# Two transformer blocks on one core: the norm factors computed on 128x4 instead of 128x512

## The chip, the cores and the metric

The kernel runs on one core of a Trainium2 chip. The metric is the device time of one execution in microseconds (us), the median over several runs; lower is better.

## The reference, cut to what matters

The program is two layers of a first block (retention, state space and forgetting attention side by side), then RWKV, memory attention, a dilated attention and four SwiGLU feed-forward networks, all for one sequence of 512 tokens of 1024 features in f32. What the change touches is the root mean square norm, which comes ahead of nearly every one of these parts:

```python
def _rmsnorm(t, gain=None):
    t32 = t.astype(jnp.float32)
    t32 = t32 * lax.rsqrt(jnp.mean(t32 * t32, axis=-1, keepdims=True) + EPS)
    ...

def swiglu_ffn(x, norm_g, w_in, w_out):
    gate, up = jnp.split(rms_norm(x, norm_g) @ w_in, 2, axis=-1)
    return (jax.nn.silu(gate) * up) @ w_out
```

Each norm needs one number per token, 1/sqrt(mean of squares + EPS): 512 numbers in all. Call it the token's factor.

## The kernel before, in words

Activations lie with the features on the 128 partitions and the tokens along the free dimension: `x` is 128 x 8 x 512. A weight tile is 128 x 1024; it is loaded into a ring of four `raw` buffers, split by ScalarE (ACT) into a rounded high part (`w_hi`, L379) and by VectorE (DVE) into the rest (`w_lo`, L386), two buffers of each, and multiplied by TensorE (PE) in `Linear.pe` (L475): for each of eight k blocks three passes of 512 columns, hi by hi, hi by lo and lo by hi. One such tile takes 24 passes. The parts of a tile are due again as soon as PE has finished the tile two ahead of it: first ACT's `w_hi`, then DVE's `w_lo`, then PE.

All instructions come from stages, each a set of generators that yield a due time. `weave` merges the generators of an engine by due time into one program per engine. So the due times fix the order, and every engine works in that order: an instruction that waits holds back all behind it on its engine.

The factor must stand on all 128 partitions, since DVE multiplies tiles of 128 x 512 by it. It is made in `Rstd` (L663), ten times over the program counting the stage `TwoNorms`:

- the squares of x (or of the mixer's output) are summed over the eight feature blocks by POOL into `square_sums` (L653, L1394), 128 x 512;
- PE multiplies them by a 128 x 128 matrix of ones (L678), which sums over the partitions and writes the sum of each token on every partition, 128 x 512, in a PSUM bank;
- DVE scales and adds EPS (L687), ACT takes the root (L699), DVE the reciprocal (L691), each on 128 x 512. The result is `rstd`.

At the start of the program the sums are taken otherwise (`Startup.pe`, L927): the eight blocks of squares are multiplied by the ones one after the other, accumulated in the bank. There, DVE also works through the eight loads of the modulation weights `ada` (`Modulation`, L1036 and L1039), PE sums these over the partitions (L1071), and then the first norm is applied (`NormIn`, L1098 and L1106) and the first weight tile can start.

`TwoNorms` (L706) makes the factor of the last norm of the first block and of the norm behind it in one go: two products by the ones (L721), then on DVE and ACT a chain of nine instructions on 128 x 512, with two roots (L764, L767) and two reciprocals (L734, L744). It runs beside four short weight tiles of the memory's keys and values (256 columns to a pass instead of 512).

In each layer of the first block `Layer` puts an `Rstd` between the state space part and the attention `Fox`; the first transposes of the attention's values (`Turns`, L1649, copied out by DVE at L1678) wait for DVE's L687 of it. At the head of layer 1 (`rstd1`) nothing else is left to do while the factor is made. The other five stand at the head of the RWKV projection, of two feed-forward networks, of the keys and of the queries; there PE goes on with the product, since the factor is applied to its result, and the first result is taken late (`NORM_LATE`).

A second group of norms, in `Ret`, works another way: L1958 multiplies the squares as the stationary operand by one column of ones, which gives 128 x 4 (a token to a partition), L1994 and L2047 take root and reciprocal on 128 x 4, and L1967 multiplies a column of this, repeated 128 times as the stationary operand, by the identity, which spreads the factors over the partitions again.

Of the kernel before, what the change touches and what calls it, by code (L numbers as in the profile page):

```python
# [147 lines left out]
N_ROUNDED = CONST["ident"][0]  # L148

# [513 lines left out]
class Rstd(Stage):  # L663

    def __init__(self, core, at, summed, dst, n=T, src=None, bank=None, in_bank=False):
        self.core, self.start, self.summed, self.dst, self.n = core, at, summed, dst, n
        self.bank = bank or core.aux[0]
        self.src = src if src is not None else core.ss[0]
        self.in_bank = in_bank  # L670
        self.total = core.share("rstd_total", 0 if in_bank else 1)
        self.meaned, self.rooted, self.made = (core.share("rstd_" + s, 1) for s in ("mean", "root", "made"))

    def pe(self, pe):
        def sums():
# [4 lines left out]
        return () if self.in_bank else (sums(),)  # L680

    def dve(self, dve):
        def factors():
            r = self.dst[:, 0:self.n]
            yield self.start + 1.0
            dve.wait_ge(*(self.summed if self.in_bank else self.total.ge(1)))
# [7 lines left out]
    def act(self, act):  # L694
        def roots():
            r = self.dst[:, 0:self.n]
            yield self.start + 1.8
            act.wait_ge(*self.meaned.ge(1))
            act.activation(r, r, ACT.Sqrt).then_inc(*self.rooted.inc())  # L699
        return (roots(),)  # L700
# [5 lines left out]
class TwoNorms(Stage):  # L706

    def __init__(self, core, at, summed, apply_at):
        self.core, self.start, self.summed, self.apply_at = core, at, summed, apply_at  # L710
        self.total, self.meaned, self.rooted, self.made, self.applied = (
            core.share("rstd_" + s, n) for s, n in (("total", 2), ("mean", 2), ("root", 2), ("made", 5),
                                                    ("applied", KD)))

    def pe(self, pe):
        def sums():
            core = self.core
# [3356 lines left out]
```

## Time and profile before

| | us |
|---|---|
| median of 3 runs | 3478.35 |
| lowest and highest of them | 3477.93, 3479.72 |
| span of the profiled execution, first to last instruction | 3482.5 |
| PE busy in it | 3349.0 |
| DVE busy in it | 1780.3 |
| ACT busy in it | 1196.0 |
| mean granted clock of PE | 0.978 of full |

The profiled execution is one of its own; of its time the span alone is known, and that is 4.15 us above the median. Times in the rows are us from the start of that span, durations of one instruction in ns where a row says min/median/max. A f32 product is recorded as two passes, so that eight products of one column stand as x16. A clock of 1.00 is 2.4 GHz, one of 0.50 is 1.2 GHz.

### The profile page before, as it was taken

Reading aid. Unit: us, or ns where it says so; the run is one execution under the profiler, and the core shown is the slowest. Engines: PE = TensorE matmul, PEld = TensorE weight load, DVE = VectorE, ACT = ScalarE, POOL = GpSimd, SP = SyncE. Lnnn points to the kernel's source line nnn. Section 1 sums busy time; section 2 is a strip of 40 time slices with the busy share of each in tenths; the row PEclk is TensorE's granted clock in tenths of the full one; section 3 lists DMA queues with packets and bytes.
Section 4 is the critical chain, followed back from the end, with each engine's and each line's share of the span. In section 5 each row is a group of like instructions: output and inputs, shape, how many; then the busy total and the mean of one; then the engine's idle time right before and its main releaser. Section 6 shows DMA issues by size and latency. Waiting matters only on the chain.

```text
span 3482.5 us, 44013 instructions
## 1 busy us (share of the span) xinstructions
PE 3349.0 (96%) x18330; PEld 2599.3 (75%) x18330; DVE 1780.3 (51%) x2532; ACT 1196.0 (34%) x1884; POOL 409.8 (12%) x318
## 2 busy tenths in 40 slices
PE   5999999899999899999999999999999999999999
PEld 4766678576677788887777777888777887678887
DVE  6854454744436743336767554434454335463433
ACT  3344432433443422224333242222353224342221
POOL 0000011000000311002322111100101011011110
PEclk8999999999999999999999999999999999899999
DMA  5631123221222333333200014332322332013332
GB/s 208 212 110 62 51 97 96 67 85 55 61 80 81 101 92 96 93 97 109 68 14 2 26 51 123 92 97 85 102 80 86 96 89 90 10 61 97 91 97 85
DMA packets 83909, 295.44 MB, mean 85 GB/s; under 512 B 9472, under 2 KB 12800, under 8 KB 81664
## 3 DMA queue, kind: packets, MB, share of 16 engines
q1 hardware_dynamic: 78384, 270.61, 25.3%
q10 hardware_dynamic: 5328, 22.02, 1.9%
q8 instruction: 146, 2.39, 0.3%
q14 instruction: 51, 0.42, 0.0%
HBM read 283.94 MB, written 8.65 MB: 84 GB/s over the span
## 4 chain that ended last, share of the span: by engine, by line
PE 83%; DVE 8%; ACT 2%; issue 1%; POOL 1%; DMA 1%; DVEq 0%; POOLq 0%; ACTq 0%
PE acc L475 66%; PE acc L1464 1%; DVE w_lo L386 1%; PE acc L3217 1%; PE acc L2443 1%; DVE square_sums L2902 1%; PE aux L3181 1%; PE aux L1745 1%; PE aux L3186 1%; PE acc L1776 1%; DMA late_ada<-in_ada 1%; ACT w_hi L379 1%; DVE ssd_ex L1366 1%; PE acc L2447 1%; PE acc L2433 1%
## 5 line engine op out<-in xcount | busy, mean ns | idle before, releaser
L475 PE MATMUL acc<-op_hi,w_hi 128*128 128x512 f32 x2624 | 1100.4, 419 | 37.1 <-DVE w_lo L386 16.6
L475 PE MATMUL acc<-op_lo,w_hi 128*128 128x512 f32 x2624 | 1041.7, 397 | 0.0
L475 PE MATMUL acc<-op_hi,w_lo 128*128 128x512 f32 x2624 | 1040.9, 397 | 0.0
L379 ACT ACTIVATE w_hi<-raw 128x1024 fp32r<-128x1024 f32 (+2 forms) x476 | 494.7, 1039 | 1581.6 <-PE acc L475 1549.6
L386 DVE TENSOR_TENSOR w_lo<-raw,w_hi 128x1024 fp32r<-128x1024 f32 (+2 forms) x476 | 576.6, 1212 | 288.5 <-ACT w_hi L379 288.1
L475 PEld LDWEIGHTS acc<-op_hi,w_hi 128*128 128x128 f32 x2624 | 495.9, 189 | 219.2 <-issue 82.4
L475 PEld LDWEIGHTS acc<-op_hi,w_lo 128*128 128x128 f32 x2624 | 496.0, 189 | 120.3
L475 PEld LDWEIGHTS acc<-op_lo,w_hi 128*128 128x128 f32 x2624 | 496.8, 189 | 115.5 <-issue 11.5
L475 PE MATMUL acc<-ffn_hi,w_hi 128*128 128x512 f32 x800 | 316.5, 396 | 0.0
L475 PE MATMUL acc<-ffn_lo,w_hi 128*128 128x512 f32 x800 | 316.1, 395 | 0.0
L475 PE MATMUL acc<-ffn_hi,w_lo 128*128 128x512 f32 x800 | 316.1, 395 | 0.0
L594 DVE SCALAR_TENSOR_TENSOR x<-acc,x 128x512 f32<-128x512 f32 x112 | 77.4, 691 | 286.8 <-PE acc L475 286.7
L815 POOL TENSOR_TENSOR ffn_gate<-ffn_gate,rstd 128x512 f32<-128x512 f32 x66 | 114.8, 1740 | 836.5 <-ACT ffn_gate L806 836.5
L795 DVE TENSOR_TENSOR ffn_product<-ffn_gate,acc 128x512 f32<-128x512 f32 x88 | 60.4, 686 | 260.3 <-PE acc L475 256.1
L475 PEld LDWEIGHTS acc<-ffn_lo,w_hi 128*128 128x128 f32 x800 | 150.2, 188 | 36.8 <-issue 0.2
L475 PEld LDWEIGHTS acc<-ffn_hi,w_hi 128*128 128x128 f32 x800 | 150.2, 188 | 36.6 <-issue 0.2
L475 PEld LDWEIGHTS acc<-ffn_hi,w_lo 128*128 128x128 f32 x800 | 150.2, 188 | 36.4
L790 DVE TENSOR_TENSOR ffn_gate<-acc,rstd 128x512 f32<-128x512 f32 x66 | 45.6, 691 | 183.9 <-PE acc L475 183.8
L1264 ACT ACTIVATE ssd_ex<-aux,ssd_ncum 128x512 f32<-128x512 f32 (+3 forms) x128 | 62.4, 522 | 85.9 <-PE aux L1450 85.9
L1366 DVE TENSOR_TENSOR ssd_ex<-ssd_ex,ssd_cb 128x1024 f32<-128x1024 f32 (+1 forms) x64 | 60.2, 949 | 47.2 <-ACT ssd_ex L1264 47.1
L815 POOL TENSOR_TENSOR ffn_gate<-ffn_gate,square_sums 128x512 f32<-128x512 f32 x22 | 40.0, 1816 | 275.4 <-ACT ffn_gate L806 275.4
L653 POOL TENSOR_TENSOR square_sums<-square_sums,squares 128x512 f32<-128x512 f32 x35 | 56.2, 1604 | 95.9 <-ACT squares L632 95.9
(578 smaller groups left out, 3901.6 us busy)
## 6 DMA issues: line engine op xcount, KB each, us to landing
raw<-in_w SPq DMA_DIRECT2D x436, 512.0 KB, 3.6
late_ada<-in_ada ACTq DMA_DIRECT2D x32, 512.0 KB, 4.4
raw<-in_w SPq DMA_DIRECT2D x32, 384.0 KB, 3.0
ada<-in_ada ACTq DMA_DIRECT2D x4, 1024.0 KB, 15.0
ada<-in_ada SPq DMA_DIRECT2D x4, 1024.0 KB, 21.9
x_mid<-x SPq DMA_DIRECT2D x16, 256.0 KB, 3.4
x<-x_mid SPq DMA_DIRECT2D x2, 2048.0 KB, 9.1
skew<-rel_rows SPq DMA_DIRECT2D x12, 192.0 KB, 3.0
```

The source lines that it names most:

```text
L379: act.activation(self.w_hi[g % 2][:, 0:k, :], self.raw[s][:, 0:k, :], ACT.Copy).then_inc(self.split_hi.handle, 1)
L386: dve.tensor_tensor(self.w_lo[g % 2][:, 0:k, :], self.raw[g % RING][:, 0:k, :], self.w_hi[g % 2][:, 0:k, :].bitcast(F32), ALU.subtract).th ...
L475: mm = pe.matmul(self.bank(s, g), w[:, k, :], a[:, k, 0:s.n], start=(k == 0 and q == 0), stop=(k == k_tiles - 1 and q == 2))
L594: dve.scalar_tensor_tensor(out=x[:, u, :], in0=bank, scalar=self.scale(u), in1=x[:, u, :], op0=ALU.mult, op1=ALU.add).then_inc(core.freed[ ...
L653: pool.tensor_tensor(core.ss[i][:, :], core.ss[i][:, :], src, ALU.add).then_inc(*self.summed.inc())
L790: dve.tensor_tensor(f.gate[:, slot, :], bank, f.rstd, ALU.mult).then_inc(freed, 1)
L795: dve.tensor_tensor(f.product[:, slot, :], f.gate[:, slot, :], bank, ALU.mult).then_inc(freed, 1)
L815: pool.tensor_tensor(f.gate[:, q % 2, :], f.gate[:, q % 2, :], f.rstd, ALU.mult).then_inc(*f.gated.inc())
L1264: act.activation(self.ex[u % self.EX][:, e, 0:n], core.aux[2 * (u % 2) + e][:, 0:n], ACT.Exp, bias=self.ncum[:, b, 2 * pair + e:2 * pair + ...
L1366: dve.tensor_tensor(ex, ex, tiled(cb[pair // 4][:, at[b]:at[b] + n], 2), ALU.mult).then_inc(*self.weighted.inc())
L1464: mm = pe.matmul(core.acc[2 + pair % 2][e * HD:(e + 1) * HD, b * P:T], self.xdt[:, b, h * SSD_DIM:(h + 1) * SSD_DIM], self.ex[u % self.EX] ...
L1745: pe.matmul(core.aux[e][:, 0:n], self.q[half[e], j, t * P:n], self.k[half[e], j, 0:n], start=True, stop=False, skip_group_check=True)
```

## The change

All ten factors are made on 128 x 4. PE multiplies the squares as the stationary operand by one column of ones, four times for the four blocks of 128 tokens; ACT takes the root with scale 1/D and EPS as its bias; DVE takes the reciprocal; PE multiplies a repeated column by the identity, four times, into the same bank; DVE copies the bank to `rstd`, 128 x 512. DVE's L687 is gone. At the start of the program the 32 one-column products accumulate in four columns. `TwoNorms` does its whole chain on 128 x 4 and spreads and copies two results. The identity is loaded in the early transfer with the ones. In the layers the attention's score stage, no longer its transposes, waits, and for the finished factor.

```diff
 class Rstd(Stage):
     def pe(self, pe):
         def sums():
             yield self.start
             pe.wait_ge(*self.summed)
-            pe.matmul(self.bank[:, 0:self.n], self.core.c("ones"), self.src[:, 0:self.n], start=True,
-                      stop=True).then_inc(*self.total.inc())
+            for t in range(NT):
+                mm = pe.matmul(bank[:, t:t + 1], self.src[:, t * P:(t + 1) * P], core.c("ones")[:, 0:1], start=True,
+                               stop=True)
+            mm.then_inc(*self.total.inc())
+        def spreads():
+            yield self.start + 2.6
+            pe.wait_ge(*self.inverted.ge(1))
+            for t in range(NT):
+                mm = pe.matmul(bank[:, t * P:(t + 1) * P], column(core.norm_small[:, t:t + 1]), core.c("ident"),
+                               start=True, stop=True)
+            mm.then_inc(*self.spread.inc())
     def act(self, act):
+            yield self.start + 1.0
+            act.wait_ge(*(self.summed if self.in_bank else self.total.ge(1)))
+            act.activation(core.norm_small[:, 0:NT], self.bank[:, 0:NT], ACT.Sqrt, scale=1.0 / D,
+                           bias=core.norm_eps[:, 0:1]).then_inc(*self.rooted.inc())
     def dve(self, dve):
-            yield self.start + 1.0
-            dve.tensor_scalar(r, self.bank[:, 0:self.n], 1.0 / D, EPS, ALU.mult, ALU.add
-                              ).then_inc(*self.meaned.inc())
+            yield self.start + 2.0
+            dve.wait_ge(*self.rooted.ge(1))
+            dve.reciprocal(core.norm_small[:, 0:NT], core.norm_small[:, 0:NT]).then_inc(*self.inverted.inc())
             yield self.start + 4.0
-            dve.wait_ge(*self.rooted.ge(1))
-            dve.reciprocal(r, r).then_inc(*self.made.inc())
+            dve.wait_ge(*self.spread.ge(1))
+            dve.tensor_copy(self.dst, self.bank[:, :]).then_inc(*self.made.inc())
...
 class TwoNorms(Stage):
+        def spreads():
+            yield self.start + 6.0
+            pe.wait_ge(*self.step.ge(5))
...
 class Startup(Stage):
-            at, n = CONST["ones"]
+            at, n = CONST["ident"][0], EARLY
             sp.dma_start(core.const[:, at:at + n], core.dram["const"][:, at:at + n]).then_inc(*self.ones.inc(16))
...
-                mm = pe.matmul(self.core.aux[0][:, :], self.core.c("ones"), self.core.squares[:, j, :],
-                               start=(j == 0), stop=(j == KD - 1))
+                for t in range(NT):
+                    mm = pe.matmul(self.core.aux[0][:, t:t + 1], self.core.squares[:, j, t * P:(t + 1) * P],
+                                   self.core.c("ones")[:, 0:1], start=(j == 0 and t == 0),
+                                   stop=(j == KD - 1 and t == NT - 1), skip_group_check=True)
...
-        fox.turn_v.ready.append(self.rstd.meaned.ge(1))
+        fox.heads.ready.append(self.rstd.ready())
...
-    rstd0 = Rstd(core, 2.9, startup.summed.ge(1), core.rstd, in_bank=True)
+    rstd0 = Rstd(core, 4.1, startup.summed.ge(1), core.rstd[:, :], in_bank=True)
```

Three places show how the order moves. First DVE at the start of the program, before (`ada_69` to `ada_73` are the first five loads of modulation weights):

```order
L1036 TENSOR_SCALAR ada_sum_77<-ada_69,cond 128x1024
L1039 SCALAR_TENSOR_TENSOR ada_sum_77<-ada_69,cond,ada_sum_77 128x1024
L1039 SCALAR_TENSOR_TENSOR ada_sum_77<-ada_70,cond,ada_sum_77 128x1024 x2
L687 TENSOR_SCALAR rstd<-aux 128x512
L1039 SCALAR_TENSOR_TENSOR ada_sum_77<-ada_71,cond,ada_sum_77 128x1024 x2
L691 RECIPROCAL rstd<-rstd 128x512
L1039 SCALAR_TENSOR_TENSOR ada_sum_77<-ada_72,cond,ada_sum_77 128x1024 x2
L1036 TENSOR_SCALAR ada_sum_78<-ada_73,cond 128x1024
```

and now:

```order
L1077 SCALAR_TENSOR_TENSOR ada_sum_77<-ada_70,cond,ada_sum_77 128x1024 x2
L1077 SCALAR_TENSOR_TENSOR ada_sum_77<-ada_71,cond,ada_sum_77 128x1024 x2
L712 RECIPROCAL norm_small<-norm_small 128x4
L1077 SCALAR_TENSOR_TENSOR ada_sum_77<-ada_72,cond,ada_sum_77 128x1024 x2
L715 COPY rstd<-aux 128x512
L1074 TENSOR_SCALAR ada_sum_78<-ada_73,cond 128x1024
```

The small reciprocal stands where the large one stood, ahead of the work on `ada_72`; the copy stands behind that work. Then DVE in `TwoNorms`, before:

```order
L731 TENSOR_SCALAR rstd<-aux 128x512
L565 TENSOR_TENSOR mem_v_141<-acc,mem_part_149 128x256
L386 TENSOR_TENSOR w_lo<-raw,w_hi 128x1024
L734 RECIPROCAL rstd<-rstd 128x512
L736 TENSOR_TENSOR square_sums<-rstd 128x512
L738 SCALAR_TENSOR_TENSOR square_sums<-aux,square_sums 128x512
L741 TENSOR_SCALAR square_sums<-square_sums 128x512
L565 TENSOR_TENSOR mem_v_141<-acc,mem_part_149 128x256
L386 TENSOR_TENSOR w_lo<-raw,w_hi 128x1024
L565 TENSOR_TENSOR mem_k_140<-acc,mem_part_149 128x256
L744 RECIPROCAL square_sums<-square_sums 128x512
L746 TENSOR_TENSOR square_sums<-rstd,square_sums 128x512
```

and now:

```order
L566 TENSOR_TENSOR mem_v_141<-acc,mem_part_149 128x256
L387 TENSOR_TENSOR w_lo<-raw,w_hi 128x1024
L769 RECIPROCAL norm_small<-norm_small 128x4
L771 TENSOR_TENSOR norm_small<-norm_small 128x4
L566 TENSOR_TENSOR mem_v_141<-acc,mem_part_149 128x256
L387 TENSOR_TENSOR w_lo<-raw,w_hi 128x1024
L775 COPY rstd<-aux 128x512
L566 TENSOR_TENSOR mem_k_140<-acc,mem_part_149 128x256
L775 COPY square_sums<-aux 128x512
L387 TENSOR_TENSOR w_lo<-raw,w_hi 128x1024
```

Between two splits `w_lo` there now stand small instructions and at most two copies. Last PE at the norm inside layer 0, before and now:

```order
L678 MATMUL aux<-square_sums,const 128x512
L475 MATMUL acc<-op_hi,w_hi 128x512
L475 MATMUL acc<-op_lo,w_hi 128x512
L475 MATMUL acc<-op_hi,w_lo 128x512
L1649 MATMUL aux<-const,fox_v 128x128 x4
L475 MATMUL acc<-op_hi,w_hi 128x512
```

```order
L683 MATMUL aux<-const,square_sums 128x1 x4
L476 MATMUL acc<-op_hi,w_hi 128x512
L476 MATMUL acc<-op_lo,w_hi 128x512
L476 MATMUL acc<-op_hi,w_lo 128x512
L1687 MATMUL aux<-const,fox_v 128x128 x4
L476 MATMUL acc<-op_hi,w_hi 128x512
L476 MATMUL acc<-op_lo,w_hi 128x512
L476 MATMUL acc<-op_hi,w_lo 128x512
L691 MATMUL aux<-const,norm_small 128x128 x4
L476 MATMUL acc<-op_hi,w_hi 128x512
```

The spreads stand behind six more weight passes and four transposes; at the five later heads nine weight passes lie between sums and spreads, in `TwoNorms` 51, at the head of layer 1 none. On ACT the root stands directly behind the squares, ahead of the next `w_hi`, at every head; in `TwoNorms` one `w_hi` stands between the two roots.

## Rows read from the trace of the kernel before

**Rows 1.** The page: busy time by engine, and the chain by engine.

```profile
PE 3349.0 (96%) x18330; PEld 2599.3 (75%) x18330; DVE 1780.3 (51%) x2532; ACT 1196.0 (34%) x1884; POOL 409.8 (12%) x318
PE 83%; DVE 8%; ACT 2%; issue 1%; POOL 1%; DMA 1%; DVEq 0%; POOLq 0%; ACTq 0%
```

**Rows 2.** By tile, `rstd`: ns min/median/max, first and last start, form.

```profile
L687 DVE TENSOR_SCALAR rstd<-aux x9: 683/691/692, 22.9 to 3114.4; 128x512 f32<-128x512 f32 x9
L699 ACT ACTIVATE rstd<-rstd x9: 617/631/633, 23.6 to 3117.5; 128x512 f32<-128x512 f32 x9
L691 DVE RECIPROCAL rstd<-rstd x9: 3343/3346/3353, 26.0 to 3118.1; 128x512 f32<-128x512 f32 x9
```

**Rows 3.** By tile, `roots`: the norms of `Ret` on 128x4.

```profile
L1994 ACT ACTIVATE roots<-sums x8: 205/206/208, 526.4 to 1114.1; 128x4 f32<-128x4 f32 x8
L2047 DVE RECIPROCAL sums<-roots x8: 166/168/170, 528.5 to 1114.6; 128x4 f32<-128x4 f32 x8
```

**Rows 4.** Chain of waits, 484 to 532 us: start, us, what.

```profile
487.83 0.86 PE aux L1926 x2
...
525.40 0.79 PE aux L1958 x8
...
530.97 0.89 PE aux L1967 x8
```

**Rows 5.** Timeline of DVE at the start: start, us, instruction, idle before.

```profile
20.41 2.60 DVE L1039 SCALAR_TENSOR_TENSOR ada_sum<-ada,cond,ada_sum 128x1024 f32<-128x1024 f32 x2 [7.02 <-DMA ada<-in_ada]
...
29.31 2.51 DVE L1039 SCALAR_TENSOR_TENSOR ada_sum<-ada,cond,ada_sum 128x1024 f32<-128x1024 f32 x2
31.73 0.74 DVE L1036 TENSOR_SCALAR ada_sum<-ada,cond 128x1024 f32<-128x1024 f32 x1
```

**Rows 6.** Timeline of PE at the start.

```profile
13.20 8.88 PE L927 MATMUL aux<-squares,const 128*128 128x512 f32 x16 [13.20 <-ACT squares L904]
...
44.06 3.57 PE L1071 MATMUL acc<-const,ada_sum 128*128 128x1 f32 x16 [8.55 <-DVE ada_sum L1039]
```

**Rows 7.** Windows: busy PE, PEld, DVE, ACT, POOL, then PEclk, DMA share, GB/s.

```profile
44.00:47.70 3.70, 3.57 (x16) 3.49 (x16) 2.30 (x4) 0.00 (x0) 0.00 (x0) 0.50 0.40 116
47.70:54.30 6.60, 4.66 (x11) 3.18 (x12) 6.44 (x11) 5.34 (x8) 0.00 (x0) 0.50 0.28 94
```

**Rows 8.** Chain of waits at the head of layer 1, 604 to 630 us.

```profile
614.17 2.09 PE aux L678 x2
...
617.67 3.37 DVE rstd L691
...
621.06 0.76 DVE squares L1098
```

**Rows 9.** Chain of waits in `TwoNorms`, 1185 to 1215 us.

```profile
1194.38 3.27 DVE rstd L734
...
1201.35 3.27 DVE square_sums L744
```

**Rows 10.** Timeline of PE in `TwoNorms`.

```profile
1201.08 0.49 PE L475 MATMUL acc<-mem_hi,w_hi 128*128 128x256 f32 x1 [3.61 <-DVE w_lo L386]
...
1206.53 0.39 PE L475 MATMUL acc<-mem_hi,w_hi 128*128 128x256 f32 x1 [0.84 <-DVE w_lo L386]
```

**Rows 11.** Timeline of ACT in `TwoNorms`.

```profile
1192.06 1.06 ACT L379 ACTIVATE w_hi<-raw 128x1024 fp32r<-128x1024 f32 x1 [1.03 <-PE acc L475]
```

**Rows 12.** Timelines in layer 0: PE's first transpose, DVE's first copy of one.

```profile
348.83 0.63 PE L1649 MATMUL aux<-const,fox_v 128*128 128x128 f32 x4 [0.19 <-DVE rstd L687]
...
349.57 0.69 DVE L1678 COPY fox_vtok<-aux 128x512 f32<-128x512 f32 x1 [0.88 <-PE aux L1649]
```

**Rows 13.** Windows at the head of a feed-forward network, columns as above.

```profile
2083.00:2098.00 15.00, 15.00 (x65) 11.70 (x64) 9.43 (x11) 6.53 (x8) 1.31 (x2) 1.00 0.27 81
```

**Rows 14.** Timelines at the queries (PE) and at the RWKV projection (POOL).

```profile
2926.73 0.47 PE L475 MATMUL acc<-op_hi,w_hi 128*128 128x512 f32 x1 [1.13 <-DVE b_q L565]
...
1596.96 2.66 POOL L2798 MEMSET x<- 128x3072 f32 x1 [10.75 <-DMA x_mid<-x]
```

More of the change, by code:

```diff
@@ L710, in __init__ @@
         self.core, self.start, self.summed, self.apply_at = core, at, summed, apply_at
[L711 to L712 removed]
+        self.total, self.rooted, self.step, self.spread, self.made, self.applied = (
+            core.share("rstd_" + s, n) for s, n in (("total", 1), ("root", 2), ("step", 5), ("spread", 2), ("made", 2),
                                                     ("applied", KD)))
     def pe(self, pe):
+        core = self.core
         def sums():
[L717 removed]
             yield self.start
@@ L725, in dve @@
+        return sums(), spreads()
     def dve(self, dve):
+        core = self.core
+        small = core.norm_small
+        first, second, both = small[:, 0:NT], small[:, NT:2 * NT], small[:, 2 * NT:3 * NT]
         def factors():
-            core = self.core
-            first, second, both = core.rstd[:, :], core.ss[0][:, :], core.ss[1][:, :]
-            yield self.start + 1.0
-            dve.wait_ge(*self.total.ge(2))
-            dve.tensor_scalar(first, core.aux[0][:, :], 1.0 / D, EPS, ALU.mult, ALU.add).then_inc(*self.meaned.inc())
@@ L740, in factors @@
-            dve.wait_ge(*self.made.ge(3))
-            dve.tensor_scalar(second, second, EPS, None, ALU.add).then_inc(*self.meaned.inc())
-            yield self.start + 9.0
-            dve.wait_ge(*self.rooted.ge(2))
-            dve.reciprocal(second, second).then_inc(*self.made.inc())
-            dve.wait_ge(*self.made.ge(4))
-            dve.tensor_tensor(both, first, second, ALU.mult).then_inc(*self.made.inc())
+            yield self.start + 2.0
+            dve.wait_ge(*self.rooted.ge(1))
@@ new lines, in factors @@
+            dve.reciprocal(first, first).then_inc(*self.step.inc())
+            dve.wait_ge(*self.step.ge(1))
+            dve.tensor_tensor(second, first, first, ALU.mult).then_inc(*self.step.inc())
+            dve.wait_ge(*self.step.ge(2))
+            dve.tensor_tensor(second, second, core.aux[0][:, NT:2 * NT], ALU.mult).then_inc(*self.step.inc())
+            yield self.start + 4.0
+            dve.wait_ge(*self.rooted.ge(2))
+            dve.reciprocal(second, second).then_inc(*self.step.inc())
@@ L748, in final_norm @@
+            dve.wait_ge(*self.step.ge(4))
+            dve.tensor_tensor(both, first, second, ALU.mult).then_inc(*self.step.inc())
+            for i, dst in enumerate((core.rstd[:, :], core.ss[1][:, :])):
+                yield self.start + 8.0 + i
+                dve.wait_ge(*self.spread.ge(i + 1))
+                dve.tensor_copy(dst, core.aux[i][:, :]).then_inc(*self.made.inc())
         def final_norm():
-            core = self.core
             for j in range(KD):
```

81 lines of the change are left out of this document (44 added, 37 removed).

## The prediction

> **What bounds the kernel now.** I began with the page's busy times: PE is busy 96% of the span, DVE 51%, ACT 34%, and the chain that ended last runs 83% over PE and 8% over DVE [rows 1]. So DVE time saved is worth nothing on average, and PE time added costs its full length wherever PE has no gap. The answer hangs on which of the ten norms sits where PE waits. For that I took the durations of the old instructions by tile [rows 2], the same forms on 128x4 from the retention norms, which already work the new way [rows 3, 4], and then each of the ten places by timeline or chain. They fall into four kinds:
>
> - the start, where DVE works from 20.41 us on without a gap [rows 5] and PE waits for it;
> - the head of layer 1, where every step of the norm is on the chain [rows 8];
> - the two norms beside the memory's keys, where DVE's two reciprocals hold back a `w_lo` each and PE idles 3.61 and 0.84 us for these [rows 10];
> - the others, where PE multiplies on. A window at the head of a feed-forward network shows PE busy 15.00 of 15.00 us [rows 13].
>
> **Prices.** Removed from DVE per norm: 0.69 (scale and EPS) and 3.35 (reciprocal); ACT's root of 0.63 becomes 0.21; the small reciprocal costs 0.17 [rows 2, 3]. A copy of 128x512 out of PSUM costs 0.69 [rows 12]. DVE saves 4.04 - 0.17 - 0.69 = 3.18 us per norm. PE at full clock: one f32 product of 512 columns is 0.86 (I take a product of the same form, L1926), four of one column 0.79, four spreads 0.89 [rows 4]. PE pays 0.79 + 0.89 - 0.86 = 0.82 us more per norm. Both new forms are rows of this kernel, so these prices are safe to some 0.1 us each.
>
> **The start.** The sums were 16 passes and took 8.88 us from 13.20 [rows 6], over at 22.1, ahead of DVE's need. They become 64 one-column passes. Which clock do they get? After 13.20 the old passes of 512 columns ran, and the granted clock was full for a while. But one-column passes have their own row: from 44.06 they fill 3.57 us without a gap, at a granted clock of 0.50 (1.2 GHz), and the clock stays at 0.50 through the next window, up to 54.3 [rows 6, 7]. So I take it that they don't raise it: 16 passes are 3.57, four such groups 14.3, and 13.9 when the three inner tails overlap. The early transfer grows by 64 KB and pushes x by about 0.15 (64 KB at the 420 GB/s that the trace shows there). Sums end at 13.35 + 13.9 = 27.25. Root and reciprocal follow with three hops of 0.03: 27.7. DVE has finished `ada_71` at about 25.6 and waits 1.8 us there, behind which all its modulation work is queued; then `ada_72` 2.51, then the copy 0.69, whose spreads (1.8 us at half clock) are hidden behind `ada_72`. The next piece starts at 30.9 instead of 31.73 [rows 5]: **-0.9 us**. If the clock rose, DVE would keep 3.18 less 0.15: that is the lower bound -3.0. The upper bound is +0.5, if a pass costs 0.235.
>
> [...]
>
> **The head of layer 1.** All of this is at half clock: L678 took 2.09 for what is 0.86 at full clock [rows 4, 8]. From 614.17: eight passes are half of 3.57, 1.8; root 0.21, reciprocal 0.17 and hops, to 616.45; spreads twice 0.89, 1.8, to 618.3; copy 0.69, to 619.1. Before, the first tile of `squares` began at 621.06: **-1.9 us**. A clock that comes back earlier could add up to -0.8, which I leave to the range.
>
> **The two norms.** The second `w_lo` there had its `w_hi` ready at about 1195.9 and ran behind the 3.27 us of the first reciprocal and three more full-width steps [rows 9]; PE stood 3.61 us, lost its clock over it, ran the next short tile with starts 0.21 apart where 0.114 is the pace before, and stood again 0.84 us for the `w_lo` behind the second reciprocal [rows 10]. With the change the second `w_lo` ends at about 1197.1. PE pays 16 one-column passes instead of 1.72 us (even) and 16 spread passes of 1.78. Two weight tiles at 2.74 each and the spreads between start the next tile at 1199.1, not 1201.08; that tile takes 2.74 at full clock, so the tile behind it starts at 1201.9 instead of 1206.53 [rows 10]. Its own `w_lo` is done at 1201.7: PE's `w_hi` at 1199.3 plus 1.06, plus 1.22, which leaves 0.2 us. **-4.6 us**. Bounds: -2.0 if only the first gap is paid back and a later split is late, -4.9 with nothing late at all. The spreads must find their columns ready: the second root waits behind the `w_hi` of 1192.06 to 1193.12 [rows 11], the last step is done at 1194.8, and the spreads come up on PE, 51 passes after the sums, at 1195.4. There is 0.6 us to spare.
>
> **Both layers' inner norm.** PE pays 0.82 and gets back the 0.19 for which its first transpose waited for DVE's scaling [rows 12]. The reciprocal does hold DVE's split, but PE had no gap over 0.1 us from it. **+0.6 twice, +1.3**. Bounds 0 and +1.7.
>
> **The heads with PE dense.** A feed-forward network twice and the keys: +0.82 three times [rows 13], **+2.5**. DVE's 3.18 less is worth nothing there, being hidden under PE, whose tiles take 5.6 us each. Bounds +1.8 and +3.
>
> **The queries and the RWKV projection.** At the queries PE stood 1.13 us because the first result could be read only behind the reciprocal [rows 14]. That wait goes, PE's 0.82 comes in its place: **-0.3**. At the RWKV projection PE waits for DVE, and DVE for POOL, whose clearing of x waits until 1596.96 for the store of x [rows 14]; that store is issued behind a weight load that needs a `w_lo` which the norm never delayed. So the date stays and hides PE's 0.82: **0**.
>
> **The sum.** -0.9 - 1.9 - 4.6 + 1.3 + 2.5 - 0.3 = **-3.9 us**. The profiled execution has a span of 3482.5, so 3478.6 by this working; the median of the runs lies 4.15 below that span, and I take the difference over to it: 3478.35 - 3.9 = **3474.4 us**. About 0.2% (7.0 us) is what a measurement of this kernel can tell from no change; the forecast lies inside that.
>
> **The rivals.**
>
> *The one-column sums do get the full clock at the start.* For it: the clock was full from 16.8 to 27 in the old run, and 64 passes last much longer than the 16 of 44.06. Against: that row [rows 6, 7]. The start gives -3.0 in place of -0.9: 3472.3.
>
> *More comes back than I count.* In the layers the chain ran over the reciprocal, the split and the copies behind it, and I call that free; and the head of layer 1 may regain its clock sooner. -0.6 per layer and -0.8, with the full start on top half of the time: 3478.35 - 7 = 3471.3.
>
> *Another split is late in the two norms.* DVE still works in order there: a copy of `rstd` stands behind a tile result that PE delivers only at 1199.3, and the next `w_lo` behind that. With 0.2 us to spare, a hop or two more and a PE that stands again give -2.0 instead of -4.6: 3477.0.
>
> *PE waits for the small reciprocal.* This ends slower. The spreads stand in PE's own order, with the weight passes queued behind them. Between sums and spreads are nine passes, 2.1 us, against 0.5 for root and reciprocal. It decides when the reciprocal comes over 2.1 us late: if ACT's root is behind a table load of 1.28 and a `w_hi` of 1.06, or DVE behind a `w_lo` of 1.22, it is 0.5 + 2.34 - 2.1 = 0.75 us per head, and 1.5 with both. At seven heads 0.75 is +5.2: 3479.6, slower than before, and with both 3484.8. Against: the order shows the root ahead of the next `w_hi` at every head, and the small reciprocal ahead of the `w_lo`.
>
> **How the numbers follow.** Forecast 0.58; full clock at the start 0.13; more comes back 0.10; a late split 0.12; PE waits 0.07. The range 3470 to 3480 holds all but the far ends of the second and the last rival. Faster by over 0.2% needs -7.0: most of the case of more, a part of the full clock, little of the forecast's own spread: 0.18. Slower by over 0.2% needs both delays of the last rival: 0.03. Within: 0.79.
>
> **What would show each step.** At the start, DVE idle some 1.8 us before a reciprocal of 0.17 at 27.5, and PE's 64 passes 0.21 us apart; starts 0.11 apart would mean the first rival. At the head of layer 1, 5.0 us from the sums' start to the first `squares`, not 6.9. In the two norms, no PE gap over 1 us behind a `w_lo` and no drop of the clock there. At the dense heads, PE still without a gap, later by 0.8. Wrong would be: a PE gap before any spread, or a `w_lo` waiting behind a copy.

## The result, and the profile after

| | before | after |
|---|---|---|
| median us (number of runs) | 3479.03 (4) | 3420.85 (4) |
| lowest, highest | 3477.93, 3481.28 | 3415.27, 3432.71 |
| ratio to before, 95% interval | | 0.9841, 0.9822 to 0.9860 |
| profiled execution: own time, span | span 3482.5 | 3432.71, 3430.7 |
| mean granted clock of it | 0.978 | 0.980 |

The change saves 58 us. The forecast was 4. Nothing of that size can lie in ten norms that cost a few us each, so the first question was where in the program the time goes. The page, to be read against [rows 1]:

```profile
PE 3310.2 (96%) x18526; PEld 2629.9 (77%) x18526; DVE 1745.3 (51%) x2533; ACT 1193.3 (35%) x1884; POOL 411.6 (12%) x318
PE 84%; DVE 8%; ACT 2%; issue 2%; POOL 1%; DMA 0%; DVEq 0%; POOLq 0%; ACTq 0%
```

PE is 39 us less busy, though it has 196 more instructions. PE's groups by line show where. Before:

```profile
L475 PE MATMUL acc<-op_hi,w_hi 128*128 128x512 f32 x2624 | 1100.4, 419 | 37.1 <-DVE w_lo L386 16.6 <-DVE op_lo L1106 11.0 <-ACT ssd_soft L1235 3.8
L475 PE MATMUL acc<-op_lo,w_hi 128*128 128x512 f32 x2624 | 1041.7, 397 | 0.0
L475 PE MATMUL acc<-ffn_hi,w_hi 128*128 128x512 f32 x800 | 316.5, 396 | 0.0
```

and after:

```profile
L476 PE MATMUL acc<-op_hi,w_hi 128*128 128x512 f32 x2624 | 1088.8, 415 | 32.7 <-DVE w_lo L387 18.3 <-DVE op_lo L1144 7.0 <-ACT ssd_soft L1273 3.8
L476 PE MATMUL acc<-op_lo,w_hi 128*128 128x512 f32 x2624 | 1029.9, 392 | 0.0
L476 PE MATMUL acc<-ffn_hi,w_hi 128*128 128x512 f32 x800 | 311.4, 389 | 0.0
```

The same passes, the same counts, and each is 4 to 7 ns shorter, also the 800 on `ffn_hi`, nearly half of which lie over 100 us away from any norm. Durations overlap here, so the pace is better read as passes in a stretch. The windows from 2150 to 2400 us, weight passes alone (columns: PE busy, PEld busy, PEclk, DMA share, GB/s), before:

```profile
2150.00:2400.00 250.00, 249.81 (x1071) 200.90 (x1070) 1.00 0.32 95
```

and after:

```profile
2150.00:2400.00 250.00, 250.00 (x1105) 207.01 (x1104) 1.00 0.30 94
```

```text
span 3430.7 us, 44407 instructions
## 1 busy us (share of the span) xinstructions
PE 3310.2 (96%) x18526; PEld 2629.9 (77%) x18526; DVE 1745.3 (51%) x2533; ACT 1193.3 (35%) x1884; POOL 411.6 (12%) x318
## 4 chain that ended last, share of the span: by engine, by line
PE 84%; DVE 8%; ACT 2%; issue 2%; POOL 1%; DMA 0%; DVEq 0%; POOLq 0%; ACTq 0%
PE acc L476 66%; PE acc L1502 1%; DVE w_lo L387 1%; PE acc L3255 1%; PE acc L2481 1%; PE aux L3219 1%; DVE square_sums L2940 1%; PE aux L1783 1%; PE aux L3224 1%; PE acc L1814 1%; ACT w_hi L380 1%; DVE ssd_ex L1404 1%; PE acc L2485 1%; PE acc L2471 1%; PE aux L1801 1%
## 5 line engine op out<-in xcount | busy, mean ns | idle before, releaser
L476 PE MATMUL acc<-op_hi,w_hi 128*128 128x512 f32 x2624 | 1088.8, 415 | 32.7 <-DVE w_lo L387 18.3
L476 PE MATMUL acc<-op_hi,w_lo 128*128 128x512 f32 x2624 | 1030.5, 393 | 0.0
L476 PE MATMUL acc<-op_lo,w_hi 128*128 128x512 f32 x2624 | 1029.9, 392 | 0.0
```

Source lines behind the costliest of these rows:

```text
L476: mm = pe.matmul(self.bank(s, g), w[:, k, :], a[:, k, 0:s.n], start=(k == 0 and q == 0), stop=(k == k_tiles - 1 and q == 2))
```

## The experiments

Runs of the kernel before stood beside each set on the same chip; their medians were 3472 to 3473 us there. Where a window is shown, it is that of 2150 to 2400 us again, weight passes alone.

### One cause at a time: the address without the change, the change without the address

The kernel before, with 64 bytes of padding (e1):

```diff
         core.rstd = core.sb("rstd", [P, T])
+        core.sb("pad", [P, 16])
```

> The kernel before with 64 unused bytes on each partition behind rstd, so that square_sums and every tile behind it lie 64 bytes higher, as in the change; no instruction differs. In the trace of before, a weight pass of 512 columns starts 233.3 ns after the last, in the trace of the change mostly 226.7 ns. Theory A (the addresses do it: the operands of the passes start at a multiple of 128 bytes now, at an odd multiple of 64 before): pace 226.7 ns, and about the time of the change plus the 3.9 us that I had worked out for the norms, 3415 to 3437 us. Theory B (the new instructions set another rhythm on TensorE, the addresses do nothing): 3479 us, pace 233.3 ns.

Measured: 3423.73 us (3414.28 to 3432.09, 4 runs), ratio 0.9851 [0.982, 0.9881], mean pace 227.58 ns.

```profile
2150.00:2400.00 250.00, 250.00 (x1105) 207.01 (x1104) 1.00 0.31 94
```

An allocation that nobody reads or writes gives the gain, with not one new instruction. The changed kernel with its two small tiles in free columns of `roots`, so that all placed tiles lie as before (e2):

```diff
-        core.norm_small, core.norm_eps = core.sb("norm_small", [P, 3 * NT]), core.sb("norm_eps", [P, 1])
+        core.norm_small, core.norm_eps = core.roots[:, 16:16 + 3 * NT], core.roots[:, 16 + 3 * NT:17 + 3 * NT]
```

> The change with its 52 bytes of small tiles put into unused columns of the tile roots, so that all other tiles keep the addresses of before; the same instructions in the same order. Theory A: the passes go back to 233.3 ns, and what is left is the norm change alone, which I forecast at 3474.4 us (3470 to 3480). Theory B: 3415 to 3433 us as the change, pace 226.7 ns.

Measured: 3477.15 us (3469.32 to 3482.54, 10 runs), ratio 1.0004 [0.9991, 1.0017], pace 233.29 ns.

```profile
2150.00:2400.00 250.00, 250.00 (x1073) 201.40 (x1073) 1.00 0.29 93
```

All ten new norms are in it and nothing is gained. Theory A holds, B falls.

### How far: 128 bytes

The changed kernel with 64 bytes more (e3), and the kernel before with 128 (e4):

```diff
+        core.sb("pad", [P, 16])   # changed kernel
+        core.sb("pad", [P, 32])   # kernel before
```

> The change with 64 more unused bytes, so that the operands of the passes start at an odd multiple of 64 bytes again, but 128 bytes above their place in before. Theory A in its form 'multiple of 128 bytes': 233.3 ns and some 3475 us, as with the small tiles in roots. Theory A in another form (some one address, or the place of the small tiles, was bad in before): 226.7 ns and 3415 to 3433 us. Theory B: 3415 to 3433 us.

> The kernel before with 128 unused bytes, operands at an odd multiple of 64 bytes as in before, 128 bytes higher. A control. Theory A, multiple of 128 bytes: 3479 us, 233.3 ns. Theory A in another form: may be 3420 to 3437 us. Theory B: 3479 us.

Measured: 3433.19 us (3428.56 to 3442.72, 4 runs), ratio 0.9882 [0.9856, 0.9908], and 3437.33 us (3433.63 to 3440.59, 4 runs), ratio 0.9891 [0.9864, 0.9917]; paces 229.34 and 229.25 ns. I had thought of a plain rule, that tiles want to begin at a multiple of 128 bytes or must not; it falls, since +128 is quick too, but less than +64.

### Period, and whose address

The operands 256 bytes later; the weights 64 later with the operands fixed; both 64 later; the upper half of the map (with `ffn_hi`, `ffn_lo`) alone 64 later:

```diff
+        core.sb("pad", [P, 64])               # e5, behind rstd

         self.piece = 0
+        self.sb("pad", [P, 16])               # e6 and e7, ahead of raw
         self.raw = [self.sb(f"raw{s}", [P, KC, P]) for s in range(RING)]
...
+        core.cond = core.roots[:, 48:48 + KD] # e6: makes room, so that the operands stay
+        core.att_small = core.roots[:, 32:44]
+        core.sb("pad2", [P, 8])

-        return self.nc.alloc_sbuf_tensor_at(name, shape, dtype, offset=self.at + int(kb * 1024))
+        return self.nc.alloc_sbuf_tensor_at(name, shape, dtype, offset=self.at + int(kb * 1024) + (64 if kb >= 0 else 0))   # e8
```

> The kernel before with 256 bytes of padding per partition, so that every placed tile and with it the operands of the weight passes lie 256 bytes later. So far: +0 gives 233.3 ns from start to start of a pass, +64 gives 227.6, +128 gives 229.3. If the pattern repeats every 256 bytes or less, this is the kernel before again: 233.3 ns, 3473 to 3479 us. If it does not (a period of 512 or more, or only the old place is slow), passes are quicker: 227 to 231 ns and 3415 to 3455 us.

> The kernel before with raw, w_hi, w_lo and the constants 64 bytes later and the operands (op_hi, op_lo, ffn_hi, ffn_lo) and square_sums at their old addresses. Theory 1, the operand's own address sets the pace: 233.3 ns per pass, 3473 to 3479 us, no change. Theory 2, the distance between operand and weight tile sets it (two reads that meet): the distance is 64 bytes off as in the padded kernel, with the other sign, so 227 to 230 ns and 3415 to 3440 us.

> The kernel before with everything in SBUF from the raw weight tiles on 64 bytes later, so that weights and operands keep their distance. Theory 1, the operand's own address: as the kernel with 64 bytes of padding ahead of the operands alone, 227.6 ns and 3415 to 3435 us. Theory 2, the distance: as before, 233.3 ns and 3473 to 3479 us.

> The kernel before with only the upper part of the placed tiles 64 bytes later: ffn_hi, ffn_lo and all that shares their room move, x, squares, op_hi and op_lo stay. If each tile's own address sets the pace of its passes: passes on ffn_hi and ffn_lo at 226.7 ns, those on op_hi and op_lo at 233.3; of some 10,280 passes 2,400 read the ffn tiles, so 2,400 x 6.6 ns = 16 us less, about 3457 to 3463 us. If what else runs beside the passes (writes of x, sums of squares, DVE and ACT in their tiles) sets it, the paces of both kinds move together: all at 233 or all at 227 to 230.

Measured: e5 3469.55 us, ratio 0.9991 [0.9976, 1.0006], 233.29 ns; e6 3470.11, 0.9994 [0.998, 1.0009], 232.64 ns; e7 3475.4, 1.0011 [0.9997, 1.0024], 233.28 ns; e8 3460.65, 0.9965 [0.9952, 0.9979], 231.62 ns in the mean.

- e5: 256 bytes later is as if nothing were moved. The pattern repeats at 256 bytes or a divisor of it, and the divisors 128 and 64 are excluded by the runs above.
- e7: the operands are 64 bytes later as in the quick kernel, but the weights moved with them, and nothing is gained. So it isn't the operand's own address.
- e6: the distance changed the other way and gave nothing, which misses what theory 2 expected there, but is no contradiction once a distance has its own pace each.
- e8: passes on `ffn_hi` and `ffn_lo` at 226.8 and 226.7 ns, on `op_hi` and `op_lo` at 233.3 and 233.2, in one kernel. 2,397 x 6.6 ns is 16 us; measured 11.4 against before's 3472.09. What moves is a property of the pair of tiles that a pass reads.

In e8's window the two kinds are mixed; 1079 lies between, as most tiles there read `op`:

```profile
2150.00:2400.00 250.00, 250.00 (x1079) 202.56 (x1080) 1.00 0.31 96
```

### The distance, tested where it must be quick

Call distance the start of `op_hi` less that of `w_hi`, modulo 256. It is 192 before, 0 in the changed kernel. The kernel that decides (e9) has the operands where they were, modulo 256, and the distance 0 by the weights alone:

```diff
+        self.sb("pad", [P, 48])               # ahead of raw: weights +192
...
+        core.sb("pad2", [P, 16])              # behind rstd: operands +256 in all
```

> The kernel before with raw, w_hi, w_lo and constants 192 bytes later and the placed tiles 256 bytes later. Moving the operands by 256 alone changed nothing (233.3 ns, 3469.6 us); moving the weights by 64 with the operands fixed, or both by 64, changed nothing or little (232.6 and 233.3). Distance theory: what counts is the distance from weight tile to operand modulo 256 bytes; it is 192 in the kernel before, 0 with the operands alone 64 later (226.7 to 227.6 ns), 64 with them 128 later (229.3), 128 in the kernel with the weights alone moved. Here it is 0 again, with the operands at their old place modulo 256: 227 to 228 ns and 3415 to 3435 us. Theory of the operand's own place, with the weights at a multiple of 128 as a second condition: 233 ns and 3465 to 3480 us.

Measured: 3421.25 us (3418.74 to 3425.4, 4 runs), ratio 0.9855 [0.984, 0.9869], pace 227.59 ns.

```profile
2150.00:2400.00 250.00, 250.00 (x1104) 207.01 (x1104) 1.00 0.32 95
```

The distance theory holds and the other falls. Beside it two finer offsets, the map 96 (e10) and 32 bytes later (e11):

> The kernel before with the placed tiles 96 bytes later (distance 32 modulo 256), between the offset that gave 227.6 ns (+64) and the one that gave 229.3 (+128). If the pace changes in steps of 64 bytes: 227.6 or 229.3. If it is graded by 32: about 228.5 ns and 3425 to 3435 us. A figure under 227 would mean that the best offset isn't a multiple of 64. If tiles that start at an odd multiple of 32 cost something by themselves, over 229.3.

> The kernel before with the placed tiles 32 bytes later (distance 224 modulo 256), between +0 (233.3 ns) and +64 (227.6). Steps of 64: one of the two. Graded: about 230.5 ns and 3440 to 3455 us.

Measured: 3475.35 us, ratio 1.0004 [0.9992, 1.0015], and 3470.8, ratio 0.9998 [0.9986, 1.0011], both at 233.22 ns. It is neither graded nor in steps: between two quick offsets (64 and 128) lies a slow one. Last the kernel with the operands 192 later (e16), whose distance is that of e6 by other means, 256 bytes apart:

> The kernel before with 192 bytes of padding ahead of the placed tiles, which makes the distance 128 modulo 256, as in the kernel whose weights alone lie 64 later (232.6 ns, 3470.1 us). If the distance is all that counts: 232.6 ns again with the same spread of single values (229, 230, 232, 237), 3465 to 3475 us. If the operand's own place adds something, another pace, 227 to 231.

Measured: 3472.52 us, ratio 0.9992 [0.9977, 1.0008], pace 232.64 ns, that of e6 to the hundredth, and in the same odd mixture (229, 230, 232, 237 or 238). The table of all of it:

| distance modulo 256 | kernels | mean ns from start to start |
|---|---|---|
| 0 | after, e1, e9 | 227.6 |
| 32 | e10 | 233.2 |
| 64 | e3, e4 | 229.3 |
| 128 | e6, e16 | 232.6 |
| 192 | before, e2, e5, e7 | 233.3 |
| 224 | e11 | 233.2 |

### Which tile is the partner

`w_lo` alone at distance 0 (e12), `raw` alone (e13), `w_hi` alone (e14), each with the operands 256 bytes later:

```diff
+        self.sb("pad", [P, 48])               # e12: between w_hi and w_lo
         self.w_lo = [self.sb(f"w_lo{s}", [P, KC, P], F32R) for s in range(2)]

+        self.sb("pad", [P, 48])               # e13: w_hi and w_lo first, then this, then raw

+        self.sb("pad", [P, 48])               # e14: ahead of w_hi
         self.w_hi = [self.sb(f"w_hi{s}", [P, KC, P], F32R) for s in range(2)]
+        self.sb("pad1", [P, 16])              # and behind it
```

> The kernel before with w_lo alone 192 bytes later and the placed tiles 256 bytes later, so that the distance modulo 256 to the operands is the old 192 for w_hi and 0 for w_lo. If a pass is slowed by the load of the weights of the next pass, which runs beside it, only the pass ahead of a w_lo pass (lo by w_hi) becomes quick, 227 ns, the two others stay at 233.3: mean 231, some 22 us less, 3448 to 3458 us. If a pass is slowed by its own weights, it is the pass hi by w_lo that becomes quick, with the same mean. If a pair of other tiles clashes (ACT's or DVE's writes), all three keep one pace.

> The kernel before with the weight tiles allocated in another order (w_hi, w_lo, 192 bytes of padding, raw) and the placed tiles 256 bytes later: the distance to the operands modulo 256 is 0 for raw and the old 192 for w_hi and w_lo. TensorE reads w_hi, w_lo and the operands, never raw. If two reads of TensorE meet, raw does not matter: 233.3 ns per pass and 3465 to 3480 us. If the writes of the loads into raw, or ACT's and DVE's reads of it, are the partner: 227.6 ns and 3415 to 3435 us.

> The counterpart of the kernel with w_lo alone moved: here w_hi lies at distance 0 modulo 256 from the operands, w_lo at the old 192. Of three passes two read w_hi as weights. If the two passes that stream beside a matching tile are quick: two of three at 227 ns, mean 229, about 3430 to 3440 us. If both halves must match before any pass is quick, as w_lo alone suggests (232.6 ns): 232 to 233 ns and 3455 to 3475 us.

Measured:

| | us, ratio | hi by w_hi | lo by w_hi | hi by w_lo |
|---|---|---|---|---|
| before | | 233.3 | 233.4 | 233.4 |
| e12, w_lo alone | 3459.0, 0.9966 [0.9953, 0.9979] | 231.4 | 232.7 | 233.7 |
| e13, raw alone | 3472.69, 0.9998 [0.9982, 1.0014] | 233.3 | 233.4 | 233.4 |
| e14, w_hi alone | 3451.06, 0.9938 [0.9917, 0.9959] | 228.4 | 229.2 | 235.8 |

(ns from the start of a pass to the next, passes on the ffn tiles.) `raw` is no partner: the loads into it and ACT's and DVE's reads of it don't matter. `w_hi` is: the two passes with `w_hi` as weights become quick and the third gets slower, so that the pace goes with the tile of a pass's own weights. How, these runs don't show. The load that runs beside a pass is that of the next pass's weights, and the two start together (e14, PE and its weight load):

```profile
2200.20 0.39 PE L477 MATMUL acc<-op_hi,w_hi 128*128 128x512 f32 x1
2200.20 0.19 PEld L477 LDWEIGHTS acc<-op_lo,w_hi 128*128 128x128 f32 x1
```

If that overlap alone set the pace, lo by w_hi, beside the load of a `w_lo` at distance 192, would have stayed slow in e14, and hi by w_lo, beside that of a `w_hi` at 0, would have become quick; neither did. Nor does `w_lo` alone mirror e14; its own pass stays slow. In both kernels `w_hi` and `w_lo` also lie at another distance from each other than in all the rest, and I can't tell these two apart. All that was expected of single passes in e12 missed, and e14's time lies between the two that had been expected. e14's gain is what its pace gives: 2.2 ns x 10,298 passes is 22 us, and 3451.06 is 20.9 below the 3471.93 of before on that chip. e12's 14.0 us are more than the 7 of its pace (232.58 ns), and that stays open.

That the partner is PE itself can also be read without another run. In the trace before, 3,292 passes run while DVE, ACT and POOL are all idle, and 6,994 beside one of them: 233.22 and 233.30 ns. In e1 it is 227.27 and 227.71. Of the idle ones, some 750 also have no DMA packet in progress: 233.24 (in e1 680, at 228.19). So nobody else has to be at work for a pass to be slow. What is left is that PE's reads of its streamed operand and of its weights disturb each other by their addresses. That is argued from what has been ruled out; no run shows the two reads at work on each other.

The Trainium skill (SBUF — State Buffer, on who interferes with whom) gives PE two read ports, one for the moving operand and one for the weights, and calls them independent. By that rule all rows of the distance table would read alike. They differ by 5.7 ns in 233, and the measurement decides.

### Undoing a part: wide norms where PE is dense

The changed kernel, with the old `Rstd` (called `RstdWide`) at the RWKV projection, two feed-forward networks and the keys:

```diff
-        Rstd(core, linear.starts[i] + NORM_AT, made.all_summed(), core.rstd[:, :])
+        (Rstd if i == queries_at else RstdWide)(core, linear.starts[i] + NORM_AT, made.all_summed(), core.rstd[:, :])
```

> The changed kernel with the old form of the norm (128x512 throughout) at the four heads where PE is dense: the RWKV projection, the two feed-forward networks, the keys. By my terms each of these gives back what PE pays more, 0.8 us (RWKV 0 to 1.4), so 2.5 to 3.5 us less than the changed kernel: 3417 to 3418 us. That is under what the times alone can tell; the ends of the w_lo splits in the trace should show it step by step: -0.8 at the head of the first feed-forward network, -0.9 at the keys, -0.4 to -0.8 at the last one. The rival, that the wide reciprocal costs as much there as PE's small products: no step over 0.3.

Measured: 3423.47 us (3407.77 to 3428.7, 5 runs), ratio 0.9847 [0.9821, 0.9874]: by the times not to be told from the changed kernel. By the ends of the `w_lo` splits, against the changed kernel: -1.3 us at the RWKV projection, -0.6 at the first feed-forward network, -0.9 at the keys, -0.4 at the last one; -3.2 in all. The four wide norms are the better ones there, as the working had it. So the best kernel of these is, by the traces, the changed one with these four undone; the times can't show 3 us.

## Why the prediction was wrong

**The step that failed** is none of the sum's terms but what the sum took for granted. The part on the change costs instructions and says nothing of its 52 bytes per partition; all tiles of PE are costed at the pace of before ("two weight tiles at 2.74 each", "whose tiles take 5.6 us each"). The change had one more part, a shift of the operands by 64 bytes, priced at nothing without a word. Alone it gains 49.2 and 51.7 us (e1, e9), over ten times the -3.9 of all the terms together. None of the rivals had it, and the range of 3470 to 3480 could not hold 3420.85. No row of before shows that the pace could be another, since it is 233 ns throughout. But addresses were there to be compared, and a range that rests on an unchanged pace of 10,000 passes hangs on a condition that should have been written down.

**The terms** can be judged in pairs of traces with the same distance: before and e2, e1 and after, e4 and e3. Each entry is how much later the new form ends the `w_lo` splits behind a head than the old one, less what it was ahead of it:

| us | forecast | e2 less before | after less e1 | e3 less e4 |
|---|---|---|---|---|
| start | -0.9 | -0.7 | -0.0 | -1.2 |
| inner norm, layer 0 | +0.6 | +0.4 | +0.4 | +0.4 |
| head of layer 1 | -1.9 | -0.6 | -1.0 | -0.9 |
| inner norm, layer 1 | +0.6 | +0.4 | +0.4 | +0.4 |
| the two norms | -4.6 | -4.7 | -3.7 | -2.8 |
| RWKV projection | 0 | +0.4 | +1.3 | +1.4 |
| first feed-forward | +0.8 | +0.9 | +0.8 | +0.8 |
| keys | +0.8 | +0.9 | +0.9 | +0.9 |
| queries | -0.3 | -0.2 | -0.6 | -0.6 |
| last feed-forward | +0.8 | +0.7 | +0.4 | +0.4 |
| sum | -3.9 | -2.4 | -1.1 | -1.1 |
| all else in the span | 0 | -9.8 | +1.7 | +7.0 |

(The forecast's entries are rounded.) The last row is the noise: between the heads the traces drift apart by up to 10 us, mostly between 2930 and 3090 us, by how long the granted clock is low there. In before, e1, the changed kernel and e3 it is low for one stretch of 30.7 us; in e2 and e4 no stretch there is longer than 10.2. That is the sign of each entry: -9.8 for e2, little for the changed kernel against e1, +7.0 for e3 against e4. Three executions of the changed kernel differ too: spans of 3430.7, 3420.6 and 3413.3 at mean clocks of 0.980, 0.984 and 0.986. Before, and e2, windows with all engines (e2 is 4 us ahead there, so that both show the same part of the program):

```profile
3010.00:3050.00 40.00, 39.14 (x186) 30.24 (x185) 19.56 (x67) 9.73 (x45) 0.00 (x0) 0.62 0.00 1
```

```profile
3010.00:3050.00 40.00, 38.49 (x258) 31.11 (x258) 23.02 (x78) 12.77 (x58) 0.00 (x0) 0.93 0.01 1
```

**The start: pace right.** After, PE and then DVE (timelines):

```profile
13.61 13.79 PE L962 MATMUL aux<-const,squares 128*128 128x1 f32 x64 [13.61 <-ACT squares L938]
27.96 2.08 PE L691 MATMUL aux<-const,norm_small 128*128 128x128 f32 x8 [0.57 <-DVE norm_small L712]
```

```profile
27.73 0.18 DVE L712 RECIPROCAL norm_small<-norm_small 128x4 f32<-128x4 f32 x1 [1.66 <-ACT norm_small L702]
27.82 2.59 DVE L1077 SCALAR_TENSOR_TENSOR ada_sum<-ada,cond,ada_sum 128x1024 f32<-128x1024 f32 x2
30.33 0.68 DVE L715 COPY rstd<-aux 128x512 f32<-128x512 f32 x1
30.93 0.74 DVE L1074 TENSOR_SCALAR ada_sum<-ada,cond 128x1024 f32<-128x1024 f32 x1
```

64 passes in 13.79 us are 0.215 apart (forecast 0.22 and 13.9), the reciprocal comes at 27.73 (27.7), DVE stood 1.66 for it (1.8), and the next piece starts at 30.93 (30.9) against 31.73 [rows 5]. DVE's 0.8 us don't always reach the first split. The rule of the Trainium skill (TensorE: Matmul & The Clock Gate, Part 1), that being busy is what releases the clock, would have had these passes at half that distance; they kept theirs for 13.8 us without a gap. One thing must be added: the granted clock of that window reads 1.00, not the 0.50 of [rows 7], at the same pace.

```profile
13.60:27.40 13.80, 13.79 (x64) 13.71 (x64) 5.14 (x4) 4.78 (x8) 0.00 (x0) 1.00 1.01 421
```

But this trace's first record of the clock begins only at 53.85 us, and up to there the column prints 1.00 for want of one. The weight passes tell what it was: 0.43 apart up to that record, 0.23 from 54.40 on.

```profile
50.26 0.63 PE L476 MATMUL acc<-op_hi,w_hi 128*128 128x512 f32 x1
50.69 0.63 PE L476 MATMUL acc<-op_lo,w_hi 128*128 128x512 f32 x1
...
54.86 0.39 PE L476 MATMUL acc<-op_hi,w_hi 128*128 128x512 f32 x1
55.09 0.39 PE L476 MATMUL acc<-op_lo,w_hi 128*128 128x512 f32 x1
```

So at 50 us PE ran at about half its later pace, as did the one-column passes (0.215 against the 0.112 of such passes at the later heads): the half clock of the forecast is borne out by these paces and not by the column.

**The head of layer 1: right at the norm, given back behind it.** The chain after, beside [rows 8]:

```profile
614.34 1.88 PE aux L683 x8
...
616.25 0.27 ACT norm_small L702
...
616.54 0.19 DVE norm_small L712
...
616.77 2.09 PE aux L691 x8
...
618.89 0.70 DVE rstd L715
...
619.61 0.76 DVE squares L1136
```

5.27 us from the sums to the first `squares`, forecast 5.0, before 6.9. Spreads took 2.09 for 1.8 and root 0.27 for 0.21: 1.6 us saved of 1.9. Then PE's passes stood 0.43 apart from 622.05 to 630.5, in e1 from 619.71 to 626.8: 1.3 us longer at half the pace, which takes 0.6 of it back. I had put the clock's part here at 0 to -0.8; it has the other sign. The clock is low for 17.1 us in both traces, from just ahead of the sums, so that a shorter norm leaves more of that stretch to the passes. (In e2 it was low for 13.7 us.)

**The two norms: right, with one hole.** DVE after:

```profile
1188.84 1.23 DVE L387 TENSOR_TENSOR w_lo<-raw,w_hi 128x1024 fp32r<-128x1024 f32 x1 [0.67 <-ACT w_hi L380]
1189.99 0.17 DVE L769 RECIPROCAL norm_small<-norm_small 128x4 f32<-128x4 f32 x1
...
1192.85 0.68 DVE L775 COPY rstd<-aux 128x512 f32<-128x512 f32 x1
...
1195.69 0.68 DVE L775 COPY square_sums<-aux 128x512 f32<-128x512 f32 x1
1196.37 1.23 DVE L387 TENSOR_TENSOR w_lo<-raw,w_hi 128x1024 fp32r<-128x1024 f32 x1
```

Both gaps of [rows 10] are gone and no later split is late: from the sums on to 1203 us no two starts on PE are over 0.3 us apart. Against before, e2 gets -4.65, forecast -4.6. But in the changed kernel PE's clock fell right behind the sums, 17 passes at 0.213 where 0.120 is the pace, and in e2 it didn't. Windows after, then e2:

```profile
1180.00:1190.00 10.00, 9.21 (x66) 9.00 (x65) 4.88 (x9) 2.57 (x4) 0.16 (x1) 0.83 0.36 112
```

```profile
1190.00:1200.00 10.00, 10.00 (x89) 10.00 (x89) 5.09 (x11) 2.57 (x4) 0.00 (x0) 1.00 0.54 159
```

17 x 0.093 is 1.6 us. I had written "no drop of the clock there"; it comes in three of the four traces with the new `TwoNorms` (the changed kernel, e3 and e15).

**The dense heads: right, with the prices nearly as forecast.** Where PE is busy at full clock, here at the queries, the spreads hold the passes up by 0.81 (forecast 0.89), and from the first of the eight one-column passes of the sums to the next weight pass it is 0.81 to 0.92 at the five heads (0.79 in [rows 4]):

```profile
2880.14 1.05 PE L691 MATMUL aux<-const,norm_small 128*128 128x128 f32 x8
2880.95 0.47 PE L476 MATMUL acc<-op_hi,w_hi 128*128 128x512 f32 x1
```

At the first feed-forward network and the keys PE pays 0.8 to 0.9, at the last network 0.4 to 0.7 for 0.8. The inner norms cost 0.4 each, inside the bounds of 0 and 0.8. **The RWKV projection: wrong.** "The date stays and hides PE's 0.82" gave 0; measured are +0.4, +1.3 and +1.4. The date doesn't stay: POOL's clearing of x itself comes later. In e1 and in the changed kernel:

```profile
1578.72 2.67 POOL L2798 MEMSET x<- 128x3072 f32 x1 [9.95 <-DMA x_mid<-x]
```

```profile
1578.48 2.67 POOL L2836 MEMSET x<- 128x3072 f32 x1 [11.37 <-DMA x_mid<-x]
```

The wait for the store of x is 1.42 us longer, and in the two other pairs 0.40 (e2, 11.15 against 10.75) and 1.46 (e3, 11.48 against 10.02), the entries of the table. Why the store lands later was not followed further.

**The rivals.** "Full clock at the start" falls by the 0.215. "A late split" falls by DVE's rows. "PE waits for the small reciprocal" falls: PE's idle time ahead of the spreads is 1.1 us over all nine places, of which 0.57 at the start and the rest at the head of layer 1. (Its second price was also added up wrong: with both delays the reciprocal comes 0.5 + 2.34 + 1.22 - 2.1 = 1.96 us late per head, not 1.5, and with DVE's delay alone not late at all.)

**The norms alone** were forecast at -3.9, a ratio of 0.9989. The times don't bear it out: e2 stands at 1.0004 of before, from 0.9991 to 1.0017, so that the forecast lies just outside. The traces give -1.1 to -2.4, inside that interval. e3 against e4, medians of four runs each, is 4.1 us less. So the new norms save 1 to 2 us by the traces, less than forecast, and nothing that the times can show.

## What to carry to other kernels

A change of the instructions is seldom only that: compare the SBUF addresses of the two kernels before arguing from instructions, and say what pace of the main loop the sum takes for granted. Where PE streams 512-column passes back to back, try offsets between operand and weight tiles (a few steps of 64 bytes, over 256): here this costs one line and gives 1.5%. And to judge a rebuilt part, compare kernels with the same addresses; the ends of a regular instruction such as `w_lo` give each place's balance to 0.1 us, where the times can't tell 7.

## What the runs showed that was not expected

- The pace of a weight pass of 512 columns depends on the distance, modulo 256 bytes, between the two tiles that it reads: 227.6 ns at 0, 229.3 at 64, 232.6 at 128, 233.3 at 192, and 233.2 at 32 and 224. Why these, and not a graded row, is open.
- The short passes of 256 columns go the other way: 114.9 ns apart before (distance 192), 113.7 in e5, 119.7 in after, e1 and e9 (distance 0). There are fewer than 200 of them, so this costs 1 us. An offset that is good for one shape isn't so for another.
- Even at distance 0 some 14% of the passes take over 229 ns; about 60% of these stand in the first block (200 to 550 and 760 to 1110 us) and from 2890 to 3050 us. The quick ones, at 226.7, keep 13 ns above 213.3, an estimate of what 512 columns take at full clock: half of the 426.7 ns between passes at half clock. What fills these 13 ns wasn't tried.
- A granted clock of 1.00 can mean that no record exists. The same pace of one-column passes, 0.22 us, stands under 0.50 in one trace and under 1.00 in another, where the first record of the clock comes at 53.85 us. Near the start of a trace the distance between passes is the better witness.
